# A two-block layer stack on one core: where two weight passes stand between the levels of the recurrent stage's inverse

## The chip, the cores and the metric

The kernel runs on one NeuronCore of one Trainium2 chip. The metric is the device time of one execution in microseconds (us). Of the kernel before, three runs took 3465.11, 3466.57 and 3469.8 us (median 3466.57). One further execution, the profiled one, took 3465.34 us.

## The reference

The program computes one block of a hybrid of dilated attention and an RWKV-7 recurrence with a feed-forward network, and then two layers of another hybrid block; x is 512 tokens by 1024 features in float32. Only the recurrence of the first block matters here. Its inputs are three projections of the same activations, each shifted in time, and its 16 heads run over the 512 tokens:

```python
rwkv_part = token_shift(proj[...], shift_mu[l])      # u + (prev - u) * mu
r_r, r_k_, r_v, dw, da, dg = jnp.split(rwkv_part, cuts, axis=-1)
...
def step(state, inp):
    r_t, w_t, k_t, v_t, a_t, b_t = inp
    sa = jnp.einsum('bhvk,bhk->bhv', state, a_t)
    state = (state * w_t[:, :, None, :] + sa[..., None] * b_t[:, :, None, :]
             + v_t[..., None] * k_t[:, :, None, :])
    return state, jnp.einsum('bhvk,bhk->bhv', state, r_t)
```

r is the receptance, k the keys, v the values. After it each head's output is normalised, gets a bonus term and is multiplied with a gate.

## The kernel before

Features lie on the 128 partitions, the 512 tokens on the free axis. The program is written out by hand for each engine: every engine works through its own list in program order, and semaphores say when an input is there. No scheduler moves anything.

**A weight pass.** `pe_features` (L582) multiplies one tile of 128 output features: 8 products over the 1024 input features, each as three matmuls of 128x512 (L574, L577, L578: weights and activations are each split into a high and a low part), so 24 matmuls. The weights stream in blocks of 8 such tiles. GpSimd (POOL) splits each block (L3293 to L3297) as soon as TensorE (PE) has begun with the block after the one whose buffer it needs, so a split begins some way into a weight pass.

**The recurrent stage.** Two heads make a pair; `pe_rwkv` (L1161), `act_rwkv` (L1710) and `dve_rwkv` (L2513) work on pair j = 0 to 7. Inside a pair the recurrence over 128-token chunks needs the inverse of a triangular matrix, which is built in five levels k = 1 to 5. In each level PE does: products z (L1192, 32 small matmuls), the transposes of the inverse so far (L729), products "normal" (L1192 with `plain`) and then the next level. VectorE (DVE) masks z (L2547) before the second products, and adds the second products to the inverse (L2562) before the next level; ScalarE (ACT) copies the transposes (L1726) before the second products.

**The chain of the pair before.** Into levels 1 to 4 of pair j the four chunk steps of pair j-1 are woven, three parts each: `first` (L1097, L1099), then ACT copies W (L1707), `second` (L1111), ACT copies U (L1707), `third` (L1122 to L1131), ACT copies the output (L1707). Pair 0 has no such chain.

**The inputs of the pair after.** For j = 0 to 6 (`more`) the three weight passes of pair j+1 stand in pair j: keys before level 1, receptance in level 2, value in level 4, the last two between `first` and `second`. ACT copies each result out of PSUM (`act_rwkv_copy`, L1636). Further work of pair j+1 has its place in the lists of the other engines:

- DVE after level 1: the cumulative sums of the decays (step 1, L2420 to L2427). In level 2, between z and the additions: the shift of the keys (step 2, L2754 and L2756), and, from pair 2 on, the mixing of pair j-2 (L2608, L2611). After level 3: step 3 (L2433, L2436). In level 4, between z and the additions: the shift of the receptance (step 4), the reciprocal of the key's length (step 8, L2444 to L2448) and step 9 (L2452). The shift of the values is at the pair's end (step 7).
- ACT in level 2, between W and U: a table load and the exponentials of the decays (`act_rwkv_decays`, L1663 to L1671). After level 3: a table load and the square root of the key's length (L1689).
- PE after level 3: the sum of squares for that length (`pe_rwkv_length`, L637).

Level 5 has the head means and the transposes of three more matrices, and after it the score maps follow (L1154, L1156). In pair 7 gate passes stand in levels 2 and 4; the change does not touch them.

Of the kernel before, what the change touches and what calls it, by code (L numbers as in the profile page):

```python
# [581 lines left out]
def pe_features(pe, ring, tag, act, k=KD, ready=None):  # L582

    tl = pe.tile(ring)
    pe.eng.wait_ge(tl.free, pe.emptied(tl))
    pe_product(pe, tl.ps, tag, *act, k, ready).then_inc(tl.full, pe.up("full_" + ring))
    return tl
# [402 lines left out]
def of(hi, lo, at=0):  # L990

    return (lambda t: hi[:, at + t, :]), (lambda t: lo[:, at + t, :])
# [60 lines left out]
def pe_rwkv_value(pe):  # L1053

    pe_features(pe, "a", "rkv", of(pe.b.h_hi, pe.b.h_lo))
# [105 lines left out]
def pe_rwkv(pe, j, chain):  # L1161

    b = pe.b
    H, AR, TF, LT = of(b.h_hi, b.h_lo), b.R_AR[j % 2], b.R_TF[j % 2], b.R_LM[:, :, 0]
    more = j + 1 < KD
    pe_features(pe, "a", "g2", of(b.s_hi, b.s_lo, 1), 1)
    pe_features(pe, "a", "gate", H)
    pe_features(pe, "d", "branch", of(b.s_hi, b.s_lo, 2), 2)
    pe.eng.wait_ge(pe.sem["rk_ready"], pe.due("rk_ready"))
    pe_plain(pe, "d", b.pair, b.R_T)  # L1170
    pe_rwkv_start(pe, lambda r, c: b.R_BH[r, c * P:(c + 1) * P], lambda r, c: AR[r, c, 0])
    tiles = [pe.tile("d") for _ in range(2)]
    pe.eng.wait_ge(tiles[1].free, pe.emptied(tiles[1]))
    for c in range(NQ):
        for half in ROWS:
            at = slice(c * P + half.start, c * P + half.stop)
            for tl, r in zip(tiles, ROWS):
                m = pe.eng.matmul(tl.ps[half, c * HD:(c + 1) * HD], AR[r, c, 0, half], b.R_BH[r, at],
                                  start=True, stop=True)
                if c == NQ - 1 and half is ROWS[1]:  # L1180
                    m.then_inc(tl.full, pe.up("full_d"))
    if more:
        pe_rwkv_keys(pe, j + 1)
    else:
        pe_features(pe, "a", "gate", H)

    def products(lhsT, rhs):
        tiles = [pe.tile("d") for _ in range(2)]
        pe.eng.wait_ge(tiles[1].free, pe.emptied(tiles[1]))
        for v in range(4):  # L1190
            for n, (row, out) in enumerate(((0, 0), (1, 1), (0, 1), (1, 0))):
                m = pe.eng.matmul(tiles[row].ps[ROWS[out], v * HD:(v + 1) * HD], lhsT(v, row, out), rhs(v, row, out),  # L1192
                                  start=True, stop=True)
                if v == 3 and n >= 2:
                    m.then_inc(tiles[row].full, pe.up("full_d"))
        return tiles[1]

    def block(t, v, row, out):
        return t[ROWS[row], 2 * v + out]

    def diagonal(src):
        tl = pe.tile("d")
        pe.eng.wait_ge(tl.free, pe.emptied(tl))
        for u in range(8):
            for r in ROWS:
                m = pe.eng.matmul(tl.ps[r, u * HD:(u + 1) * HD], src[r, u], b.ident[r, r], start=True, stop=True)
        m.then_inc(tl.full, pe.up("full_d"))
        return tl

    def corner(out, lhsT, rhs):  # L1210
        tl = pe.tile("a")
        pe.eng.wait_ge(tl.free, pe.emptied(tl))
        for u in range(8):
            m = pe.eng.matmul(tl.ps[out, u * HD:(u + 1) * HD], lhsT(u), rhs(u), start=True, stop=True)
        m.then_inc(tl.full, pe.up("full_a"))
        return tl

    for k in range(1, 6):
        c = k - 1 if chain and k <= NQ else None
        if k == 1:  # L1220
            pe.eng.wait_ge(pe.sem["t_ready"], pe.due("t_ready"))
        else:
            pe.eng.wait_ge(normal.free, pe.taken(normal))
        z = products(lambda v, row, out: LT[ROWS[row], 2 * v + out, ROWS[row]], lambda *at: block(b.R_TN, *at))
        inverse = pe_turned(pe, [b.R_TN[:, 2 * v:2 * v + 2].rearrange("p u t -> p (u t)") for v in range(4)])
        if c is not None:
            chain.first(c)
        if k == 2 and more:
            pe_rwkv_receptance(pe)
        if k == 4 and more:  # L1230
            pe_rwkv_value(pe)
        if k in (2, 4) and not more:
            pe_features(pe, "a", "gate", H)
        if k == 5:
            if j:
                pe_rwkv_mean(pe)
        if c is not None:
            chain.second(c)
        pe.eng.wait_ge(inverse.free, pe.taken(inverse))
        pe.eng.wait_ge(z.free, pe.taken(z))  # L1240
        normal = products(lambda *at: block(b.R_TW, *at), lambda *at: block(b.R_Z, *at))
        if k == 5:
            for src in (b.R_V, b.R_BH, b.R_KH):
                turned = pe_turned(pe, [src[:, q * P:(q + 1) * P] for q in range(NQ)])
            pe_rwkv_maps(pe, j, (0, 1))
        if c is not None:
            chain.third(c)
        if k == 3 and more:
            pe_rwkv_length(pe)
    upper, lower = ROWS  # L1250
    pe.eng.wait_ge(normal.free, pe.taken(normal))
    z = corner(lower, lambda u: LT[upper, u, lower], lambda u: b.R_TN[upper, u])
    last = diagonal(b.R_TN)
    maps = pe_rwkv_maps(pe, j, (2, 3))
    pe.eng.wait_ge(last.free, pe.taken(last))
    pe.eng.wait_ge(z.free, pe.taken(z))
    last = corner(upper, lambda u: b.R_Z[lower, u], lambda u: TF[lower, u, HD:])
    if j:
        pe_rwkv_variance(pe)
    return PeChain(pe, j, (turned, maps, last))  # L1260
# [368 lines left out]
def act_rwkv_copy(a, n):  # L1629


    if n - 1 > 0:
        a.eng.wait_ge(a.sem["shifted"], a.value("shifted", n - 1))
    a.eng.wait_ge(a.sem["full_a"], a.due("full_a"))
    a.eng.wait_ge(a.sem[a.last], a.own())
    a.eng.activation(a.b.R_U[:, n % 2, 1:], a.bank(), ACT.Copy).then_inc(a.sem["free_a"], a.up("free_a"))  # L1636
    a.eng.wait_ge(a.sem[a.last], a.own())
    a.eng.sem_inc(a.sem["u_ready"], a.up("u_ready"))
# [71 lines left out]
def act_rwkv(a, j):  # L1710
    b = a.b
    W, U, Y = b.R_WU[:, 0], b.R_WU[:, 1], [b.R_Y[:, c * P:(c + 1) * P] for c in range(NQ)]
    more = j + 1 < KD
    a.eng.wait_ge(a.sem["full_a"], a.due("full_a"))
    a.eng.wait_ge(a.sem[a.last], a.own())
    a.eng.activation(b.R_G[j % 3], a.bank(), ACT.Copy).then_inc(a.sem["free_a"], a.up("free_a"))
    act_first_gate(a, b.x[:, j])
    if more:
        act_rwkv_keys(a, j + 1)
    else:  # L1720
        a.eng.wait_ge(a.sem["rk_ready"], KD)
        act_late_gate(a, 0)
    for k in range(1, NQ + 2):
        a.eng.wait_ge(a.sem["full_a"], a.due("full_a"))
        a.eng.wait_ge(a.sem[a.last], a.own())
        a.eng.activation(b.R_TW, a.bank().rearrange("p (u t) -> p u t", u=8), ACT.Copy).then_inc(a.sem["free_a"], a.up("free_a"))  # L1726
        if k > NQ:
            continue
        if j:
            act_rwkv_chunk(a, W)  # L1730
        if k == 2 and more:
            act_rwkv_decays(a)
            act_rwkv_copy(a, 2 + 3 * (j + 1) + 1)
        if k == 4 and more:
            act_rwkv_copy(a, 2 + 3 * (j + 1) + 2)
        if k in (2, 4) and not more:
            act_late_gate(a, k // 2)
        if j:
            act_rwkv_chunk(a, U)
            act_rwkv_chunk(a, Y[k - 1])  # L1740
        if k == 2 and more:
            act_rwkv_squares(a, j + 1)
        if k == 3 and more:
            act_rwkv_length(a)
    for dst in (b.R_VN, b.R_BN, b.R_KN):
        a.eng.wait_ge(a.sem["full_a"], a.due("full_a"))
        a.eng.wait_ge(a.sem[a.last], a.own())
        a.eng.activation(dst, a.bank().rearrange("p (c n) -> p c n", c=NQ), ACT.Copy)\
            .then_inc(a.sem["free_a"], a.up("free_a"))
    if j:  # L1750
        act_rwkv_centered(a)
    for part, dst in ((slice(HD, P), b.R_Z[HD:P]), (slice(0, HD), b.R_TF[j % 2][0:HD, :, HD:])):
        a.eng.wait_ge(a.sem["full_a"], a.due("full_a"))
        a.eng.wait_ge(a.sem[a.last], a.own())
        a.eng.activation(dst, a.bank()[part].rearrange("p (u t) -> p u t", u=8), ACT.Copy)\
            .then_inc(a.sem["free_a"], a.up("free_a"))
    if j:
        act_rwkv_deviation(a)
# [1627 lines left out]
```

## Time and profile before

| what | value |
|---|---|
| median of 3 runs | 3466.57 us |
| profiled execution | 3465.34 us |
| span of the profile | 3463.4 us |
| mean granted TensorE clock | 0.978 |
| PE busy | 3247.9 us (94%) |
| DVE busy | 2009.3 us (58%) |
| POOL busy | 1674.6 us (48%) |
| ACT busy | 1055.9 us (30%) |
| chain that ended last, by engine | PE 75%, DVE 16%, ACT 5% |
| level 1 of pair 0 to level 1 of pair 7 | 288.94 to 740.81 us |

The span runs from the first to the last instruction; the 1.9 us between it and the execution's own time lie around the program. The recurrent stage is where PE is least the bound: its list, DVE's and ACT's wait for each other level by level.

### The profile page before, as it was taken

What the parts mean: (1) busy time and instruction counts of PE and PEld (TensorE: products, weight loads), DVE (VectorE), ACT (ScalarE), POOL (GpSimd) and SP (SyncE); (2) the same over time, 40 slices, a digit from 0 to 9 for tenths busy, and PEclk for the clock granted to TensorE, in tenths of its full rate; (3) what the DMA queues carried; (4) which work ended last, traced back from release to release, by engine and by line L of the source; (5) the groups of instructions that cost most, each with busy time, mean ns of one, the idle gap of its engine ahead of it and who ended that gap; (6) DMA issues with size and microseconds to landing.
All of it is one profiled execution on the core that took longest, in us unless ns stands there. A gap on an engine that the chain in (4) does not pass through costs nothing.

```text
span 3463.4 us, 52617 instructions
## 1 busy us (share of the span) xinstructions
PE 3247.9 (94%) x19342; PEld 2566.8 (74%) x19342; DVE 2009.3 (58%) x2727; ACT 1055.9 (30%) x1970; POOL 1674.6 (48%) x1323
## 2 busy tenths in 40 slices
PE   7988999899999999899999999999989899999999
PEld 4756777777888887576777788877657677788887
DVE  5647677765566545624645666656552635586556
ACT  2142333322121113543534321112551535231112
POOL 3423322225476664244344666655226263576665
PEclk9998999999999999999999999999999999999999
DMA  5431111112232221012121232222112121222222
GB/s 206 165 121 44 44 38 38 38 38 67 91 100 96 95 95 61 31 55 67 54 69 62 85 98 92 97 86 80 36 37 92 37 86 44 85 90 93 97 96 92
DMA packets 71657, 268.36 MB, mean 77 GB/s; under 512 B 7840, under 2 KB 7968, under 8 KB 68384
## 3 DMA queue, kind: packets, MB, share of 16 engines
q1 hardware_dynamic: 69152, 260.73, 22.6%
q10 hardware_dynamic: 2304, 4.83, 0.4%
q8 instruction: 140, 2.29, 0.3%
q14 instruction: 61, 0.50, 0.0%
HBM read 263.44 MB, written 2.10 MB: 77 GB/s over the span
## 4 chain that ended last, share of the span: by engine, by line
PE 75%; DVE 16%; ACT 5%; issue 2%; DMA 1%; POOL 0%; DVEq 0%; SPq 0%; ACTq 0%; POOLq 0%
PE psum_a L574 10%; PE psum_a L578 10%; PE psum_a L577 10%; PE psum_d L637 5%; PE psum_d L574 5%; PE psum_d L577 5%; PE psum_d L578 5%; PE psum_a L729 3%; PE psum_d L832 2%; PE psum_a L600 2%; PE psum_a L603 2%; PE psum_a L604 2%; PE psum_a L759 1%; PE psum_a L763 1%; PE psum_a L762 1%
## 5 line engine op out<-in xcount | busy, mean ns | idle before, releaser
L3297 POOL TENSOR_TENSOR w_lo<-raw,w_hi 128x1024 fp32r<-128x1024 f32 x440 | 1114.3, 2532 | 36.7
L3293 POOL TENSOR_TENSOR mark<-mark 128x1 f32<-128x1 f32 x438 | 105.5, 241 | 1712.7 <-PE psum_a L574 866.7
L574 PE MATMUL psum_a<-h_hi,w_hi 128*128 128x512 f32 x1712 | 676.7, 395 | 0.0
L578 PE MATMUL psum_a<-h_hi,w_lo 128*128 128x512 f32 x1712 | 669.1, 391 | 0.0
L577 PE MATMUL psum_a<-h_lo,w_hi 128*128 128x512 f32 x1712 | 668.9, 391 | 0.0
L3294 POOL TENSOR_SCALAR w_hi<-raw 128x1024 fp32r<-128x1024 f32 x440 | 471.2, 1071 | 33.8 <-DMA raw<-in_weights 33.8
L574 PEld LDWEIGHTS psum_a<-h_hi,w_hi 128*128 128x128 f32 x1712 | 323.1, 189 | 78.1 <-issue 11.2
L577 PEld LDWEIGHTS psum_a<-h_lo,w_hi 128*128 128x128 f32 x1712 | 323.1, 189 | 68.0 <-issue 1.9
L578 PEld LDWEIGHTS psum_a<-h_hi,w_lo 128*128 128x128 f32 x1712 | 322.7, 189 | 68.0
L574 PE MATMUL psum_d<-split,w_hi 128*128 128x512 f32 x848 | 331.1, 390 | 9.5 <-DVE x L3044 6.7
L577 PE MATMUL psum_d<-split,w_hi 128*128 128x512 f32 x848 | 330.0, 389 | 0.0
L578 PE MATMUL psum_d<-split,w_lo 128*128 128x512 f32 x848 | 330.0, 389 | 0.0
L574 PEld LDWEIGHTS psum_d<-split,w_hi 128*128 128x128 f32 x848 | 159.2, 188 | 47.3 <-issue 13.1
L578 PEld LDWEIGHTS psum_d<-split,w_lo 128*128 128x128 f32 x848 | 159.2, 188 | 33.1
L577 PEld LDWEIGHTS psum_d<-split,w_hi 128*128 128x128 f32 x848 | 159.2, 188 | 32.7
L637 PE MATMUL psum_d<-arena 64*128 64x512 f32 (+4 forms) x480 | 158.7, 579 | 12.2 <-DVEq L2844 6.9
L759 PE MATMUL psum_a<-h_hi,w_hi 128*128 128x256 f32 x416 | 123.8, 297 | 0.0
L729 PE MATMUL psum_a<-const,arena 128*128 128x128 f32 x820 | 117.2, 282 | 2.8 <-DVEq L2973 1.6
L1858 ACT ACTIVATE arena<-arena,col 128x512 f32<-128x512 f32 (+5 forms) x144 | 104.3, 724 | 47.7 <-DVE col L2644 26.4
L763 PE MATMUL psum_a<-h_hi,w_lo 128*128 128x256 f32 x416 | 117.6, 283 | 0.0
L762 PE MATMUL psum_a<-h_lo,w_hi 128*128 128x256 f32 x416 | 117.5, 283 | 0.0
L729 PEld LDWEIGHTS psum_a<-const,arena 128*128 128x128 f32 x820 | 92.7, 143 | 31.1 <-issue 20.0
(394 smaller groups left out, 5713.9 us busy)
## 6 DMA issues: line engine op xcount, KB each, us to landing
raw<-in_weights SPq DMA_DIRECT2D x440, 512.0 KB, 3.4
plain<-in_ada SPq DMA_DIRECT2D x20, 1024.0 KB, 7.2
arena<-in_ada SPq DMA_DIRECT2D x4, 1024.0 KB, 17.5
x<-in_x SPq DMA_DIRECT2D x1, 2048.0 KB, 12.8
x<-in_x ACTq DMA_DIRECT2D x1, 2048.0 KB, 10.7
out<-x SPq DMA_DIRECT2D x8, 256.0 KB, 3.7
arena<-in_pe ACTq DMA_DIRECT2D x2, 512.0 KB, 3.6
const<-in_const ACTq DMA_DIRECT2D x1, 906.0 KB, 9.4
```

The lines of the kernel that those rows point to most:

```text
L574: m = pe.eng.matmul(dst, wh, hi(t), start=t == 0, stop=False)
L577: pe.eng.matmul(dst, wh, lo(t), start=False, stop=False)
L578: m = pe.eng.matmul(dst, wl, hi(t), start=False, stop=t == k - 1)
L637: pe.eng.matmul(tl.ps[0:lhsT.shape[1], 0:rhs.shape[1]], lhsT, rhs, start=True, stop=True)\
L729: m = pe.eng.transpose(tl.ps[:, q * P:(q + 1) * P], s, pe.b.ident)
L759: m = pe.eng.matmul(tl.ps[:, cols], wh, b.h_hi[:, t, cols], start=t == 0, stop=False)
L762: pe.eng.matmul(tl.ps[:, cols], wh, b.h_lo[:, t, cols], start=False, stop=False)
L763: m = pe.eng.matmul(tl.ps[:, cols], wl, b.h_hi[:, t, cols], start=False, stop=t == KD - 1)
L1858: a.eng.activation(u.x, u.x, ACT.Exp, bias=u.neg, scale=1.0 if u.scale is None else u.scale, accum_out=u.sum)\
L3293: eng.tensor_tensor(b.mark[:, 1:2], b.mark[:, 0:1], b.mark[:, 0:1], ALU.add)
L3294: eng.tensor_scalar(hi, b.raw[:, s], 1.0, 0.0, ALU.mult, ALU.add).then_inc(sig["w_high"], 1)
L3297: eng.tensor_tensor(lo, b.raw[:, s], hi.bitcast(F32), ALU.subtract).then_inc(sig["w_ready"], 1)
```

## The change

Receptance's pass goes from level 2 to level 1, value's from level 4 to level 3, in PE's list; the two copies go with them in ACT's list. The decays stay in level 2. DVE's list is not changed, and no instruction is added or removed. The order of the weights in memory is the same, since receptance still comes before value.

```diff
@@ -1225,9 +1225,9 @@
         inverse = pe_turned(pe, [b.R_TN[:, 2 * v:2 * v + 2].rearrange("p u t -> p (u t)") for v in range(4)])
         if c is not None:
             chain.first(c)
-        if k == 2 and more:
+        if k == 1 and more:
             pe_rwkv_receptance(pe)
-        if k == 4 and more:
+        if k == 3 and more:
             pe_rwkv_value(pe)
         if k in (2, 4) and not more:
             pe_features(pe, "a", "gate", H)
@@ -1730,8 +1730,9 @@
             act_rwkv_chunk(a, W)
         if k == 2 and more:
             act_rwkv_decays(a)
+        if k == 1 and more:
             act_rwkv_copy(a, 2 + 3 * (j + 1) + 1)
-        if k == 4 and more:
+        if k == 3 and more:
             act_rwkv_copy(a, 2 + 3 * (j + 1) + 2)
         if k in (2, 4) and not more:
             act_late_gate(a, k // 2)
```

PE's list at level 4 of pair 1 (the level begins with the products z, L1192; L1097 and L1099 are `first`, L1111 is `second`). Before, the value pass follows `first`:

```order
L1192 MATMUL psum_d<-arena 64x64 x16
L729 MATMUL psum_a<-const,arena 128x128 x4
L1097 MATMUL psum_a<-arena 128x128
L1099 MATMUL psum_a<-arena 128x64 x2
L574 MATMUL psum_a<-h_hi,w_hi 128x512
L577 MATMUL psum_a<-h_lo,w_hi 128x512
L578 MATMUL psum_a<-h_hi,w_lo 128x512
```

and of the change, at the same place:

```order
L1192 MATMUL psum_d<-arena 64x64 x16
L729 MATMUL psum_a<-const,arena 128x128 x4
L1097 MATMUL psum_a<-arena 128x128
L1099 MATMUL psum_a<-arena 128x64 x2
L1111 MATMUL psum_a<-arena 128x64 x2
L1192 MATMUL psum_d<-arena,plain 64x64 x16
L1128 MATMUL psum_a<-arena 128x128
```

The pass's 24 matmuls, of which the first three stand in the first piece, are gone from level 4; they now stand between L1099 and L1111 of level 3. The same happens to receptance's pass between levels 2 and 1.

ACT's list at levels 1 and 2 of pair 1 (L1726 copies the transposes, L1707 the chunk results, L1636 a weight pass's result, L1663 to L1671 are the decays). Before:

```order
L1707 ACTIVATE arena<-psum_a 128x128 x3
L1726 ACTIVATE plain<-psum_a 128x512
L1707 ACTIVATE arena<-psum_a 128x128
L1663 ACT_TABLE_LOAD
L1663 ACTIVATE arena<-arena,col 128x128 x4
L1666 ACTIVATE arena<-col 128x4
L1668 ACTIVATE col<-col 128x4
L1671 ACTIVATE arena<-arena,col 128x128 x4
L1636 ACTIVATE arena<-psum_a 128x512
L1707 ACTIVATE arena<-psum_a 128x128 x2
```

and of the change:

```order
L1707 ACTIVATE arena<-psum_a 128x128
L1636 ACTIVATE arena<-psum_a 128x512
L1707 ACTIVATE arena<-psum_a 128x128 x2
L1726 ACTIVATE plain<-psum_a 128x512
L1707 ACTIVATE arena<-psum_a 128x128
L1663 ACT_TABLE_LOAD
L1663 ACTIVATE arena<-arena,col 128x128 x4
L1666 ACTIVATE arena<-col 128x4
L1668 ACTIVATE col<-col 128x4
L1671 ACTIVATE arena<-arena,col 128x128 x4
L1707 ACTIVATE arena<-psum_a 128x128 x2
```

The copy L1636 moved from behind the decays in level 2 to between W and U in level 1; U and the output of level 2 (the last L1707) stand directly behind the decays in both, but for that copy.

## Rows read from the trace of the kernel before

**Rows 1.** Page, part 4: the chain that ended last, by engine.
```profile
PE 75%; DVE 16%; ACT 5%; issue 2%; DMA 1%; POOL 0%; DVEq 0%; SPq 0%; ACTq 0%; POOLq 0%
```

**Rows 2.** Stretches view, level 1 of pair 6, and sum over pairs 1 to 6.
```profile
core 0: us, PE busy (x) PEld busy (x) DVE busy (x) ACT busy (x) POOL busy (x), PEclk, DMA share, GB/s
...
680.16:684.95 4.79, 4.13 (x90) 3.50 (x89) 2.95 (x6) 1.75 (x4) 0.64 (x1) 1.00 0.32 111
sum 28.73, PE 24.76 PEld 20.97 DVE 13.62 ACT 10.50 POOL 8.10; mean PE 4.13 PEld 3.49 DVE 2.27 ACT 1.75 POOL 1.35
```

**Rows 3.** The same, level 3 of pair 6, and sum over pairs 1 to 6.
```profile
695.51:701.60 6.09, 5.72 (x95) 4.27 (x95) 3.85 (x11) 2.83 (x7) 0.00 (x0) 1.00 0.20 75
sum 36.76, PE 34.19 PEld 25.50 DVE 21.98 ACT 17.72 POOL 0.50; mean PE 5.70 PEld 4.25 DVE 3.66 ACT 2.95 POOL 0.08
```

**Rows 4.** The same, level 2: pair 1, and sum over pairs 1 to 6.
```profile
358.23:368.49 10.26, 9.92 (x119) 8.37 (x117) 6.11 (x15) 6.95 (x16) 3.68 (x3) 1.00 0.03 10
...
sum 62.13, PE 59.66 PEld 50.23 DVE 50.69 ACT 42.02 POOL 23.16; mean PE 9.94 PEld 8.37 DVE 8.45 ACT 7.00 POOL 3.86
```

**Rows 5.** The same, level 4: pairs 0 and 3, and sum over pairs 0 to 6.
```profile
304.80:317.85 13.05, 7.38 (x94) 5.94 (x93) 12.19 (x12) 1.79 (x3) 4.38 (x3) 0.90 0.13 41
...
503.66:513.76 10.10, 9.55 (x114) 7.93 (x113) 9.24 (x12) 3.33 (x7) 3.88 (x3) 1.00 0.12 39
...
sum 82.04, PE 64.66 PEld 53.52 DVE 76.03 ACT 21.78 POOL 27.04; mean PE 9.24 PEld 7.65 DVE 10.86 ACT 3.11 POOL 3.86
```

**Rows 6.** Timeline, PE, pair 6, levels 1 and 2.
```profile
start us, us, engine line op out<-in xcount [idle before <-releaser]
...
681.28 0.56 PE L1099 MATMUL psum_a<-arena 128*128 128x64 f32 x4
682.50 0.66 PE L1111 MATMUL psum_a<-arena 128*128 128x64 f32 x4 [0.66 <-ACT arena L1707]
...
686.29 0.56 PE L1099 MATMUL psum_a<-arena 128*128 128x64 f32 x4
686.65 0.48 PE L574 MATMUL psum_a<-h_hi,w_hi 128*128 128x512 f32 x1
...
692.23 0.56 PE L1111 MATMUL psum_a<-arena 128*128 128x64 f32 x4
```

**Rows 7.** Timeline, ACT, pair 6, level 2.
```profile
687.31 1.28 ACT L1663 ACT_TABLE_LOAD   x1
...
690.83 1.71 ACT L1671 ACTIVATE arena<-arena,col 128x128 f32<-128x128 f32 x4
692.65 0.60 ACT L1636 ACTIVATE arena<-psum_a 128x512 f32<-128x512 f32 x1
693.42 0.28 ACT L1707 ACTIVATE arena<-psum_a 128x128 f32<-128x128 f32 x1 [0.17 <-ACTq L1638]
```

**Rows 8.** Timeline, DVE, pair 6, levels 2 and 4.
```profile
691.67 2.74 DVE L2611 TENSOR_TENSOR plain<-arena 128x512 f32<-128x512 f32 x1
...
703.66 0.69 DVE L2754 TENSOR_TENSOR arena<-arena 128x512 f32<-128x512 f32 x1
...
705.71 3.35 DVE L2446 RECIPROCAL arena<-arena 128x512 f32<-128x512 f32 x1
```

**Rows 9.** Timeline, PE, pair 6, level 3 and start of level 5.
```profile
696.95 0.56 PE L1099 MATMUL psum_a<-arena 128*128 128x64 f32 x4
697.87 0.66 PE L1111 MATMUL psum_a<-arena 128*128 128x64 f32 x4 [0.37 <-ACT arena L1707]
...
711.99 0.32 PE L1192 MATMUL psum_d<-arena 64*64 64x64 f32 x5 [0.68 <-DVE arena L2562]
```

**Rows 10.** Waits view, PE, 288 to 735 us: total, times, longest.
```profile
PE psum_d L1192 <- DVE arena L2562: 18.9, 11, 5.7
```

**Rows 11.** Timeline, POOL, pair 6, level 2.
```profile
689.36 0.19 POOL L3293 TENSOR_TENSOR mark<-mark 128x1 f32<-128x1 f32 x1 [8.55 <-PE psum_a L574]
...
691.18 2.69 POOL L3297 TENSOR_TENSOR w_lo<-raw,w_hi 128x1024 fp32r<-128x1024 f32 x1
```

**Rows 12.** Stretches view, pair 0, levels 1 and 2.
```profile
288.94:292.65 3.71, 1.98 (x69) 1.53 (x68) 1.69 (x4) 1.20 (x2) 0.00 (x0) 1.00 0.42 141
292.65:301.09 8.44, 7.38 (x93) 5.94 (x93) 7.20 (x12) 6.45 (x14) 3.93 (x3) 1.00 0.11 31
```

**Rows 13.** The same, first products of level 5, pairs 1, 4 and 5.
```profile
385.68:388.00 2.32, 2.32 (x54) 1.49 (x58) 0.99 (x3) 0.60 (x1) 0.00 (x0) 1.00 0.30 120
...
577.57:581.02 3.45, 3.45 (x39) 1.83 (x39) 0.85 (x2) 0.60 (x1) 0.00 (x0) 0.57 0.19 74
643.33:646.76 3.43, 3.43 (x39) 2.19 (x39) 0.85 (x2) 0.60 (x1) 0.00 (x0) 0.57 0.00 0
```

**Rows 14.** The same, level 5 to the gate pass, pairs 2 and 3.
```profile
451.39:464.67 13.28, 12.48 (x181) 9.13 (x181) 8.12 (x15) 4.07 (x7) 0.00 (x0) 0.87 0.09 35
513.76:525.48 11.72, 10.92 (x181) 8.37 (x181) 8.12 (x15) 4.07 (x7) 0.00 (x0) 1.00 0.04 14
```

## The prediction

> **What bounds the kernel now.** I read the chain of waits by engine first. Over the whole program PE carries 75% of it, but DVE has 16% and ACT 5% [rows 1], and the change touches only the recurrent stage, so the next view is that of stretches, cut at the start of each level's products z. The levels of pairs 1 to 6 are very unlike. A level without a weight pass is short: level 1 has 4.79 us in pair 6 and 28.73 us over six pairs [rows 2], level 3 has 6.09 us [rows 3] (36.76 us over the six; it also holds the length sum). Level 2, with receptance's pass, takes 10.26 us in pair 1 and 62.13 us over six [rows 4]; level 4, with value's, 10.10 to 13.05 us and 82.04 us over pairs 0 to 6 [rows 5]. The pass itself is 5.58 us (686.65 to 692.23 in [rows 6]).
>
> If the pass were all that makes levels 2 and 4 long, moving it would be neutral. So the question is what else is in them, and there the timelines of ACT and DVE decide.
>
> Level 2: ACT does the table load and the decays from 687.31 to 692.54 (690.83 + 1.71), and only then copies receptance's result (692.65) and U (693.42) [rows 7]. PE's pass ends at 692.23 [rows 6]. The two run side by side and end within 0.4 us of each other: either alone would make the level nearly as long.
>
> Level 4: DVE has, between its two visits to PSUM for the inverse, the shift, the reciprocal of 3.35 us and three more operations [rows 8]. Here DVE ends later than PE even with the pass in place: the next level's z waits 0.68 us for DVE's additions in pair 6 [rows 9], and the waits view has 18.9 us of waits on these additions in the stage, the longest 5.7 us [rows 10]. In DVE's busy time the same is seen: 76.03 of 82.04 us [rows 5]. Level 4 is a DVE level; the pass is hidden in it completely.
>
> Levels 1 and 3, where the passes go, have almost nothing to hide them: PE is busy 4.13 of 4.79 us in level 1 [rows 2] and 5.72 of 6.09 in level 3 [rows 3], and the idle time that a pass there could fill is the wait for W before `second`, 0.66 us in level 1 [rows 6] and 0.37 us in level 3 [rows 9].
>
> **The change part by part**, for pairs 1 to 6 at full clock first.
>
> Level 1 gains a pass. Between the starts of `first` and `second` lie 1.22 us now (681.28 to 682.50); with a pass between them it is 5.94 us (686.29 to 692.23) [rows 6], so +4.72 us. The copy of receptance stands before U on ACT, which makes `third` wait about 0.2 us more. +4.9 us each, 29.4 us for six. Behind the wait on ACT is queued only `third` and the next z.
>
> Level 3 gains the other one: 0.92 us (696.95 to 697.87, [rows 9]) becomes 5.94, +5.02, and 0.2 for the copy: +5.2 us each, 31.2 for six. Nothing else of DVE or ACT stands in these levels that the pass could cover; step 1 and step 3 on DVE come after the additions, which wait for PE's second products, so they start late by the same amount.
>
> Level 2 loses its pass, but ACT's decays keep their place between W and U. They depend on the cumulative sums, which start after level 1's additions as before. U now comes directly behind them, at 692.65 in place of 693.42 in pair 6: 0.77 us earlier. So level 2 goes from 10.26 to 9.49 us, and 6 x 9.49 = 56.9 against 62.13: -5.2 us. DVE's path through the level is shorter: masks, shift and mixing without a stall, then the additions, done some 7.7 us after the level's start, so it isn't the one that ends it. As bounds from other rows: no gain at all (10.26), and a bare level 1 (4.79), the latter only if the decays were not in the way, which the order of ACT's list excludes.
>
> Level 4 loses its pass too, and DVE's list is unchanged. The length is that of DVE alone. Pair 3 has it without a stall: 10.10 us [rows 5]. In the other pairs DVE's operations on SBUF sit out POOL's split of a weight block: L2611 takes 2.74 us in [rows 8] where L2754, an operation of the same shape, takes 0.69, and POOL's L3297 ran from 691.18 to 693.87 [rows 11]. The Trainium skill, "SBUF — State Buffer", section "SBUF: two separate sides", calls the port pair that the two engines share an exclusive lock, held for the whole instruction; the trace agrees, since L2611 ends 0.54 us after L3297 and not in proportion to it. A split begins inside a weight pass: here at 689.36, 2.7 us after the pass began, when POOL had waited 8.55 us for PE, and it took 4.5 us to the end of L3297. With the pass in level 3 it falls mostly before level 3's additions, where DVE waits for PE anyway. So I take 10.10 us for all six: 60.6 against 82.04 - 13.05 = 68.99, -8.4 us. Bounds: no return (0) and this.
>
> Pair 0 has no chain, so the pass stands between transposes and second products. Level 1: 3.71 us becomes 8.44, as its level 2 is now [rows 12]: +4.7. Level 2: nothing waits for a U; it is a bare level of 3.71 us, plus about 1.4 by which the cumulative sums hold up DVE's masks, plus about 0.8 by which the key shift (0.69 and 0.75 us) outlasts the second products: 5.9 instead of 8.44, -2.5. Level 3: like level 1, +4.7. Level 4: its 13.05 us are 2.95 above pair 3's [rows 5]; most of that is stalls of DVE, I take -2.7. Together +4.2.
>
> Sum at full clock: 29.4 + 31.2 - 5.2 - 8.4 + 4.2 = +51.2 us.
>
> The clock. PE would now stand idle for about 3.9 us in level 2 (from the end of the second products, some 4.1 us into the level, to `third` at 8.0) and about 5 us in level 4 (from `third`, done after 5.0 us, to 10.1). Before level 5 PE already waits for DVE now. After the shorter waits (pairs 1, 3, 6; 0.68 us in pair 6, [rows 9]) the granted clock stayed at 1.00, that is 2.4 GHz. After the longer ones (pairs 0, 2, 4, 5; up to 5.7 us, [rows 10]) it fell to half, 1.2 GHz: over the first products of level 5 the mean is 1.00 in pair 1 and 0.57 in pairs 4 and 5 [rows 13]. What a fall costs is in [rows 14]: level 5 and what follows takes 13.28 us at a clock of 0.87 (pair 2), 11.72 us at 1.00 (pair 3), so 1.5 us for one fall. New falls: six after the idle time of level 2, which slow the start of level 3, and three in level 5 (pairs 1, 3, 6; the others have paid already). 9 x 1.5 = 13.5 us. Bounds: none, 0; twice as long at half clock each, 27.
>
> The Trainium skill, "TensorE: Matmul & The Clock Gate", section "What's actually happening", says that the throttled state is the default and activity releases it, so a kernel pays for gaps between its matmuls beyond the gaps themselves. A count of PE's work alone, which is the same before and after, would leave the 13.5 us out; the four falls named above agree with the page.
>
> DMA, SP and POOL: the passes keep their order, so the same blocks are loaded and split, only earlier inside a pair; POOL's 8.55 us of waiting before its split [rows 11] are time in hand. Nothing. Pair 7 and all that follows only moves.
>
> Total: 51.2 + 13.5 = 64.7 us. Against the profiled execution's own time, 3465.34 us, that is 3530.0 us. The three timed runs have their median 1.2 us higher, well inside their spread of 4.7, so I leave it at 3530.
>
> **The rivals.**
>
> A. The clock doesn't fall in level 2, or the fall is over before the pass starts, and level 5 pays little more: 51.2 us, 3516. For it: the idle time of level 2 is broken by short products. Against: the waits before level 5 of pairs 4 and 5, shorter than 3.9 us, were enough [rows 13]. 17%.
>
> B. POOL's splits catch DVE again, in step 1 or in the start of level 4, and the clock stays low for longer: the 8.4 us don't come back and the clock costs up to 27: 51.2 + 8.4 + 20 = 80, 3545. For it: the idle time of 5 us in every pair would be as long as pair 0's of 5.7, the longest in the stage now [rows 10]. 15%.
>
> C, the other side. The decays and DVE's operations would end early enough, and the pass was what ended levels 2 and 4. Then each of these levels falls by a full pass, 14 x 5.58 = -78 us in pairs 0 to 6; levels 1 and 3 give 29.4 + 31.2 + 9.4 = +70: 8 us faster, 3457, and below that as far as the 18.9 us of waits for DVE shrink. It decides at one place: whether `third` of level 2 starts within 1 us of the second products' end, or stands behind L1671. For it is only that PE is 75% of the chain; against it are the ACT rows of level 2 and the DVE rows of level 4. 2%.
>
> D. The exchange is nearly neutral, because in levels 1 and 3 the passes fill idle time that the view of stretches doesn't show, PE's busy time being modelled. Then within 7 us of 3466. It would need some 4 us of idle time in each of these levels, where PE's rows leave under 1. 2%.
>
> The forecast, 3530, has the rest, 64%.
>
> **How the numbers follow.** A measurement of this kernel can tell 0.2%, 7 us, from no change. All of the forecast, A and B are far on the slow side: slower 96%; same 2% from D, faster 2% from C. The range leaves out C and D and the far tails: the lower end is A less some 6 us for levels that hide more than I count, 3510; the upper end is B, 3547.
>
> **What would show each step right or wrong.** Level 1 of pairs 1 to 6 at 9.7 us and level 3 at 11.3 us (or more where the clock is half). Level 2 at about 9.5 us, with an idle time before L1122 of more than 3 us released by ACT's L1707, behind L1671. Level 4 at 10.1 us with the wait of L1192 for L2562 at 5 us in each of six pairs, over 30 us in total. DVE operations of 2.7 us gone from level 4. A granted clock of about 0.5 at the start of levels 3 and 5. The forecast is wrong if level 2 falls under 8 us, if level 4 falls under 9, or if the change of the time lies outside pairs 0 to 6.

## The result, and the profile after

The changed kernel takes 3537.35 us (median of 4 runs, 3535.89 to 3540.16); the kernel before, run beside it, 3465.84 us. The ratio is 1.0207, with a 95% interval of 1.0190 to 1.0225: 2% slower. The forecast was 3530 with a range of 3510 to 3547. The profiled span grew from 3463.4 to 3535.5 us, the mean granted clock fell from 0.978 to 0.968, and PE's share of the chain by engine stayed at the 75% of [rows 1]. All of the loss lies in pairs 0 to 6: from level 1 of pair 0 to level 1 of pair 7 it is 523.9 us, against 451.9 before (288.94 to 740.81).

Changed kernel, stretches of one level each. The columns are those of [rows 2]. First level 1 of pair 6, then levels 2 to 5 of pair 3; each sum and mean is over pairs 1 to 6.

```profile
739.95:749.61 9.66, 9.49 (x114) 7.94 (x113) 3.19 (x6) 2.35 (x5) 4.23 (x4) 1.00 0.22 67
sum 57.95, PE 56.94 PEld 47.60 DVE 15.02 ACT 14.10 POOL 28.71; mean PE 9.49 PEld 7.93 DVE 2.50 ACT 2.35 POOL 4.79
...
519.92:530.55 10.63, 5.88 (x94) 4.88 (x92) 7.59 (x18) 6.34 (x15) 0.00 (x0) 0.84 0.05 21
sum 63.81, PE 35.34 PEld 29.32 DVE 44.73 ACT 38.04 POOL 0.91; mean PE 5.89 PEld 4.89 DVE 7.46 ACT 6.34 POOL 0.15
...
530.55:543.22 12.67, 12.50 (x120) 10.14 (x119) 3.13 (x9) 3.60 (x8) 3.59 (x3) 0.87 0.14 43
sum 75.07, PE 73.78 PEld 59.60 DVE 19.20 ACT 21.35 POOL 21.45; mean PE 12.30 PEld 9.93 DVE 3.20 ACT 3.56 POOL 3.58
...
543.22:553.06 9.84, 4.20 (x89) 3.49 (x88) 9.02 (x11) 2.73 (x6) 0.00 (x0) 0.89 0.01 2
sum 60.04, PE 25.16 PEld 20.94 DVE 54.76 ACT 16.66 POOL 0.00; mean PE 4.19 PEld 3.49 DVE 9.13 ACT 2.78 POOL 0.00
...
553.06:566.92 13.86, 13.06 (x180) 9.70 (x181) 8.12 (x15) 4.07 (x7) 0.00 (x0) 0.83 0.01 1
sum 82.60, PE 77.14 PEld 57.27 DVE 48.83 ACT 24.39 POOL 0.00; mean PE 12.86 PEld 9.54 DVE 8.14 ACT 4.07 POOL 0.00
```

Read them against [rows 2] to [rows 5]. Level 1 doubled, from 28.73 to 57.95 us, and is PE from end to end. Level 2 lost 24 us of PE's work (59.66 to 35.34) and got no shorter: 62.13 to 63.81. Level 4 lost 32 us of PE's work (64.66 - 7.38 = 57.28 in pairs 1 to 6 of [rows 5], now 25.16) and gave back 9. Pair 3's granted clock was 1.00 in levels 2 to 5 before; it is now 0.84, 0.87, 0.89 and 0.83.

Changed kernel, waits view of PE, 289 to 807 us (released by; total, times, longest).

```profile
PE psum_d L1192 <- DVE arena L2563: 41.2, 9, 7.3
PE psum_d L1122 <- ACT arena L1707: 24.4, 18, 3.8
```

The first, L2562 before, was 18.9 us in [rows 10]. The second is `third` waiting for ACT's U. Both waits stand in the timeline of PE in pair 3 (columns as in [rows 6]).

```profile
523.44 0.69 PE L1192 MATMUL psum_d<-arena,plain 64*64 64x64 f32 x32 [0.52 <-issue]
527.92 0.79 PE L1122 MATMUL psum_d<-arena 128*128 128x128 f32 x2 [3.79 <-ACT arena L1707]
528.50 0.63 PE L1123 MATMUL psum_d<-arena 128*128 128x128 f32 x2
...
553.06 1.13 PE L1192 MATMUL psum_d<-arena 64*64 64x64 f32 x32 [5.04 <-DVE arena L2563]
```

PE stands idle for 3.79 us in level 2 and for 5.04 us before level 5. What released it is in the other two timelines of the same pair: ACT's decays up to 527.49 and U directly behind them, and DVE's list of level 4.

```profile
525.79 1.70 ACT L1671 ACTIVATE arena<-arena,col 128x128 f32<-128x128 f32 x4
527.59 0.28 ACT L1707 ACTIVATE arena<-psum_a 128x128 f32<-128x128 f32 x1
```

```profile
547.09 3.35 DVE L2447 RECIPROCAL arena<-arena 128x512 f32<-128x512 f32 x1
550.48 0.75 DVE L2449 SCALAR_TENSOR_TENSOR arena<-arena,par 128x512 f32<-128x512 f32 x1
551.27 0.69 DVE L2453 TENSOR_TENSOR arena<-arena 128x512 f32<-128x512 f32 x1
552.06 0.95 DVE L2563 TENSOR_TENSOR arena<-arena,psum_d 128x256 f32<-128x256 f32 x2
```

Changed kernel, stretches of pair 3 that follow the idle time of level 2, and then the start of level 5.

```profile
524.20:527.90 3.70, 0.00 (x0) 0.00 (x0) 3.29 (x6) 3.32 (x10) 0.00 (x0) 0.89 0.00 0
527.90:531.30 3.40, 3.38 (x42) 2.83 (x46) 0.64 (x2) 0.53 (x2) 0.00 (x0) 0.50 0.00 0
531.30:534.70 3.40, 3.40 (x30) 3.14 (x23) 0.85 (x2) 1.35 (x3) 0.00 (x0) 0.62 0.02 5
534.70:543.22 8.52, 8.35 (x74) 6.25 (x73) 2.28 (x7) 1.73 (x4) 3.59 (x3) 1.00 0.20 62
553.06:556.50 3.44, 3.44 (x38) 2.19 (x38) 0.85 (x2) 0.60 (x1) 0.00 (x0) 0.50 0.00 0
556.50:559.90 3.40, 3.40 (x51) 2.76 (x52) 1.53 (x3) 1.20 (x2) 0.00 (x0) 0.81 0.02 5
```

After the idle time the clock is at half, 1.2 GHz, for all of the first 3.4 us and three quarters of the next ((1 - 0.62) x 2). The idle stretch before it, at 0.89, holds another 0.8 us of it ((1 - 0.89) x 2 x 3.70). The half clock covers `third` of level 2 and the beginning of level 3, whose first pass matmul starts at 533.66 (PE's timeline of this pair). A fall in [rows 13] was shorter: 0.57 over 3.45 us is 3.0 us at half, and the next 3.4 us had a mean of 0.94.

### The profile page after: what moved, and what is told of

The parts are those of the page before. It is cut to its first block, busy times and chain, and to the rows that moved or that the text cites. A ratio compares the mean times of both kernels' runs of the same rounds, so it can differ in the third digit from the quotient of the medians.

```text
span 3535.5 us, 52617 instructions
## 1 busy us (share of the span) xinstructions
PE 3268.5 (92%) x19342; PEld 2582.8 (73%) x19342; DVE 1989.1 (56%) x2727; ACT 1055.9 (30%) x1970; POOL 1671.2 (47%) x1323
## 4 chain that ended last, share of the span: by engine, by line
PE 75%; DVE 16%; ACT 5%; issue 2%; DMA 1%; POOL 0%; DVEq 0%; SPq 0%; ACTq 0%; POOLq 0%
PE psum_a L574 10%; PE psum_a L577 10%; PE psum_a L578 10%; PE psum_d L637 5%; PE psum_d L574 5%; PE psum_d L577 4%; PE psum_d L578 4%; PE psum_a L729 3%; PE psum_d L832 2%; PE psum_a L600 2%; PE psum_a L603 2%; PE psum_a L604 2%; PE psum_a L759 1%; PE psum_a L763 1%; PE psum_a L762 1%
## 5 line engine op out<-in xcount | busy, mean ns | idle before, releaser
L3298 POOL TENSOR_TENSOR w_lo<-raw,w_hi 128x1024 fp32r<-128x1024 f32 x440 | 1112.4, 2528 | 36.7
## 6 DMA issues: line engine op xcount, KB each, us to landing
arena<-in_ada SPq DMA_DIRECT2D x4, 1024.0 KB, 17.5
```

What stands on the lines that cost most here:

```text
L3298: eng.tensor_tensor(lo, b.raw[:, s], hi.bitcast(F32), ALU.subtract).then_inc(sig["w_ready"], 1)
```

## The experiments

Ratios are to the kernel before, run on the same chip, with 95% intervals. It had a median of 3467.73 us beside the first four and 3468.51 us beside the last two. Each experiment was one kernel. Where an experiment is said to be some us below the change, that is the difference of the two medians. The kernel before took 1.9 and 2.7 us more beside the experiments than beside the changed kernel; set off against it, the three gains of 18.6, 24.2 and 24 us below are 20.5, 26.1 and 26.8.

**Receptance alone, and value alone.** The first keeps `if k == 4 and more` for value's pass and copy. The second is the kernel before with value's two lines changed:

```diff
-        if k == 4 and more:
+        if k == 3 and more:
             pe_rwkv_value(pe)
```

> Only receptance's pass is moved (level 2 to 1); value's stays in level 4. Theory T (a pass is free only beside a long queue of DVE or ACT, and idle time of PE lowers the clock): level 1 of pairs 1 to 6 at 9.66 us (+29 over six), level 2 at 10.6 (+2), level 3 at 7.5 because it starts at half clock (+9), level 4 unchanged at 11.5 on average, pair 0 +2: about +42 us, 3508. Rival N (the levels trade the pass evenly, level 2 falls by 5.6 us): within 5 us of before, 3466, and the loss of the whole change then lies with value's pass.

> Only value's pass is moved (level 4 to 3); receptance's stays in level 2. Theory T: level 3 of pairs 1 to 6 at 11.3 us at full clock (+31), level 4 at 9.85 (-9), level 5 +6 by the clock, pair 0 +3: about +31 us, 3497, and with the run of receptance alone the two sum to the whole change's 71.5 us within 5. Rival N (level 4 falls by a whole pass): within 5 us of before.

Measured: receptance alone 3509.2 us, ratio 1.0120 (1.0104 to 1.0137), +41.5 us; value alone 3496.0 us, 1.0090 (1.0073 to 1.0107), +28.3 us. Together +69.7 against the whole change's +71.5, well within the intervals: the halves add up, and both came out as expected (3508 and 3497). In receptance alone the half clock at the start of level 3 cost less than the 9 us expected: 42.86 against 36.76 us, +6.1. (The profiled execution of the first was its shortest, 3502.03 us.) Its levels 2 and 4, sums over pairs 1 to 6:

```profile
sum 63.82, PE 35.40 PEld 29.32 DVE 44.76 ACT 38.05 POOL 0.91; mean PE 5.90 PEld 4.89 DVE 7.46 ACT 6.34 POOL 0.15
...
sum 68.96, PE 57.25 PEld 47.58 DVE 63.41 ACT 20.00 POOL 22.66; mean PE 9.54 PEld 7.93 DVE 10.57 ACT 3.33 POOL 3.78
```

Value alone, levels 3 and 4:

```profile
sum 67.77, PE 66.33 PEld 52.10 DVE 23.60 ACT 21.03 POOL 21.99; mean PE 11.05 PEld 8.68 DVE 3.93 ACT 3.50 POOL 3.66
...
sum 60.06, PE 25.16 PEld 20.94 DVE 54.80 ACT 16.69 POOL 0.00; mean PE 4.19 PEld 3.49 DVE 9.13 ACT 2.78 POOL 0.00
```

Level 2 is the changed kernel's to 0.01 us without value's move, and level 4 its to 0.02 us without receptance's. With value's pass still in level 4 DVE is busy 63.41 us there, with it in level 3 54.80: 8.6 us of sitting out POOL's splits, nearly the whole return of level 4 (68.96 - 60.06 = 8.9). And level 3 alone, with no idle time before it in level 2, is 67.77 us where the whole change has 75.07.

**What holds level 2.** ACT's decays move on to level 3, between W and value's copy, so that the pass covers them:

```diff
-        if k == 2 and more:
+        if k == 3 and more:
             act_rwkv_decays(a)
```

> The whole change, and ACT's decays (a table load and ten exponentials, 5.3 us) moved from level 2 to level 3, between W and the copy of the values, beside value's pass. Theory T (the decays between W and U are what holds level 2): U comes 3 us into level 2, DVE's additions at 7.6 us become its end, level 2 at 7.7 in place of 10.6, and level 3 at 11.3 in place of 12.5 if the clock holds: about -25 us against the change, 3512. Rival V (DVE's queue of masks, shift and mixing holds level 2): level 2 stays above 10 us, 3537. Rival P (it is PE's own products at half clock): level 2 stays above 9.

Measured: 3518.74 us, 1.0149 (1.0132 to 1.0166), 18.6 us below the change. Stretch of level 2 in pair 3 and its sum, then two level 3's, of pairs 5 and 6:

```profile
511.15:518.77 7.62, 4.71 (x94) 3.97 (x92) 6.68 (x16) 2.43 (x6) 0.00 (x0) 1.00 0.07 28
sum 44.80, PE 28.27 PEld 23.81 DVE 39.26 ACT 13.85 POOL 0.90; mean PE 4.71 PEld 3.97 DVE 6.54 ACT 2.31 POOL 0.15
...
662.78:677.19 14.41, 13.96 (x118) 11.22 (x118) 4.32 (x12) 7.51 (x17) 3.58 (x3) 0.77 0.11 38
...
741.34:752.67 11.33, 11.05 (x119) 8.71 (x119) 4.16 (x12) 7.52 (x17) 3.58 (x3) 1.00 0.14 48
```

Level 2 fell by 19 us over six pairs: its length was the decays on ACT. The next bound is DVE, seen in PE's timeline of this kernel:

```profile
518.77 0.89 PE L1192 MATMUL psum_d<-arena 64*64 64x64 f32 x32 [1.95 <-DVE arena L2563]
```

The size was missed by some 7 us. Expected was that level 3 would be spared the half clock everywhere (6 x 11.33 = 68.0 us; it took 73.91). It was in pairs 1, 4 and 6 (11.33 us). In pairs 2, 3 and 5 it was not (12.7 to 14.4 us), after a wait of only 1.94 or 1.95 us; pairs 4 and 6 had the same wait and kept their clock.

**What holds level 4.** The reciprocal of the key's length is left out of the computation; a multiplication by a constant stands in its place:

```diff
-        v.eng.reciprocal(b.R_SW, b.R_SW)
+        v.eng.tensor_scalar(b.R_SW, b.R_SW, 1.0 / 256, None, ALU.mult)
```

> The whole change with the reciprocal of the key's length replaced by a multiplication with 1/256 (the reciprocal is left out of the computation): 0.43 us in place of 3.35 on DVE in level 4. Theory T (DVE's queue sets the length of level 4): level 4 at 6.9 in place of 9.85 us in all seven pairs, -20 us, and up to -12 more if the shorter idle time spares level 5 the fall of the clock: 3505 to 3517. Rival C (the chain W, U through ACT, or PE, sets it): level 4 falls by less than 1 us, 3530 or more.

Measured: 3513.17 us, 1.0132 (1.0116 to 1.0149), 24.2 us below the change. Stretches of level 4 and level 5 in pair 3 with their sums:

```profile
530.68:537.60 6.92, 4.19 (x90) 3.49 (x89) 6.10 (x11) 2.73 (x6) 0.00 (x0) 0.99 0.01 2
sum 42.52, PE 25.16 PEld 20.94 DVE 37.24 ACT 16.68 POOL 0.00; mean PE 4.19 PEld 3.49 DVE 6.21 ACT 2.78 POOL 0.00
...
537.60:550.81 13.21, 12.41 (x181) 9.32 (x181) 8.12 (x15) 4.07 (x7) 0.00 (x0) 0.88 0.01 1
sum 82.64, PE 77.17 PEld 57.47 DVE 48.86 ACT 24.40 POOL 0.00; mean PE 12.86 PEld 9.58 DVE 8.14 ACT 4.07 POOL 0.00
```

Each level 4 lost 2.92 us (9.84 to 6.92), as DVE's list did: it is a DVE level. That a shorter wait would spare level 5 the half clock was wrong: 82.64 us, as in the changed kernel (82.60), after this wait in PE's timeline:

```profile
537.60 0.71 PE L1192 MATMUL psum_d<-arena 64*64 64x64 f32 x16 [2.12 <-DVE arena L2563]
```

The seven level 4's gave 20.4 us. Another 4.2 came from the level 3's (81.60 against 85.84 us over pairs 0 to 6), which the edit does not touch: their pass follows the same wait in level 2 (10.64 us again in pairs 1 to 6), but the half clock in them was shorter (granted 0.90 to 0.97 in pairs 1 to 6, 0.86 to 0.90 in the changed kernel). So the price of a fall was not the same in the two executions; why is open.

**What the clock costs.** The changed kernel with matmuls in PE's idle time whose result nobody reads: three of 128x512 before `third` waits for U in level 2 of pairs 1 to 6 (shown here), and, not shown, four before level 5's products wait for DVE in pairs 0 to 6.

```diff
+            for _ in range(3):
+                pe.eng.matmul(new.ps, b.ident, b.const[:, C_MASK4:C_MASK4 + T], start=True, stop=True)
         pe.eng.wait_ge(self.u.free, pe.taken(self.u))
```

> The whole change, and matmuls that nothing reads in PE's idle time of pairs 1 to 6: three of 128x512 before the third part's wait for U in level 2 (some 3 us), and in pairs 0 to 6 four before the wait for DVE's additions at the start of level 5 (some 4 us). Theory T (idle time lowers the clock, and that is worth over 20 us of the 71.5): the granted clock stays at 1.00 in levels 2 to 5, level 2 at 9.5 us (-7 over six), level 3 at 11.2 (-8), level 5 to the gate pass at 11.7 (-12), pair 0 -5: about -32 us against the change, 3505. Rival K (the clock falls in any case or costs nothing, since the others are waited for): no less than 3530. Rival F (the fillers are too long and delay what stands behind them): above 3540.

Measured: 3513.2 us, 1.0127 (1.0111 to 1.0143), 24 us below the change. Stretches of level 2 in pair 2, then of levels 2, 3 and 5 in pair 3:

```profile
440.75:451.24 10.49, 8.91 (x100) 5.68 (x99) 8.21 (x18) 6.34 (x15) 0.91 (x1) 0.84 0.16 52
...
512.25:521.71 9.46, 7.48 (x100) 5.03 (x98) 7.60 (x18) 6.35 (x15) 0.00 (x0) 1.00 0.06 23
521.71:532.86 11.15, 10.98 (x121) 8.67 (x119) 3.13 (x9) 3.61 (x8) 3.59 (x3) 1.00 0.15 48
...
542.71:554.43 11.72, 10.92 (x181) 8.37 (x181) 8.12 (x15) 4.07 (x7) 0.00 (x0) 1.00 0.01 3
```

The wait is still there, and mostly filled: PE is busy 7.48 us instead of 5.88 in level 2 of pair 3, and still idle for 1.01 us before `third`. The six pairs' levels 2, 3 and 5 take 57.79, 67.14 and 71.29 us instead of 63.81, 75.07 and 82.60. That is 25.3 us. The clock stays at 1.00 in all six level 3's, in five of the level 2's (9.46 us each) and in level 5 of pairs 2 to 6; level 5 of pair 1 has 0.97. The exception is level 2 of pair 2. There PE had waited 0.44 us before `second` and 1.14 us before the second products (0.52 us in the other five pairs), and the clock was at half under the fillers themselves:

```profile
445.51 4.54 PE L1122 MATMUL psum_d<-const 128*128 128x512 f32 x6
```

The same row is 2.84 us in pair 3. At half clock the fillers outlasted the wait and made the level 1.03 us longer, which is what rival F had named, in one place of thirteen. The gain is 8 us short of the 32 expected. Half of that is pair 0, expected at -5: its wait in level 2 got no filler, its level 3 still ran at 0.76 (10.83 us), and only 1.1 us came back in its level 5.

**The other way round: the kernel before, with less of DVE in level 4.** If level 4 is DVE's even with the pass in it, work should leave DVE's list there. The last operation of step 8 (0.75 us) and step 9 (0.69 us) move behind level 5's additions:

```diff
-            for step in (4, 8, 9):
+            for step in (4, 8):
...
+        if k == 5 and more:
+            dve_rwkv_input(v, j + 1, 9)
```

> The kernel before, without the change: on DVE the product that ends step 8 and step 9 (0.75 and 0.69 us, both inputs of the pair after) moved from level 4 to behind level 5's additions, where DVE waits about 1.1 us for the first score maps. Theory T (level 4 is as long as DVE's queue in it): the waits before level 5 shorten by up to 1.5 us each, 7 to 8 us over seven pairs, and three falls of the clock may go (4.5 us): 3455 to 3460. Rival M (what leaves level 4 delays the maps by the same amount): 3466, the same. Rival S (the operations meet POOL's splits or hold up the maps and ACT behind them): above 3468.

Measured: 3451.03 us (median of 5), ratio 0.9955 (0.9941 to 0.9969): 17.5 us faster than the kernel before, and the only version that beats both. Stretch of level 4 in pair 1 (five of the six pairs have 9.64 or 9.65, pair 5 has 11.41), and its sum:

```profile
436.36:446.00 9.64, 9.47 (x113) 7.93 (x112) 7.79 (x10) 3.06 (x6) 2.49 (x3) 1.00 0.01 3
sum 59.62, PE 56.92 PEld 47.56 DVE 49.57 ACT 18.62 POOL 21.34; mean PE 9.49 PEld 7.93 DVE 8.26 ACT 3.10 POOL 3.56
```

PE is now busy 9.47 of 9.64 us where before it waited (10.10 without a stall, up to 12.91 with one). Level 4 came down from 68.99 to 59.62 us, as far as the exchange brought it, but with the pass still inside. DVE's busy time in these levels fell by 14.3 us (63.84 to 49.57), of which 8.6 are the two operations' own; the other 5.6 are waits for splits that just these two had sat out (L2448 took up to 2.47 us in place of 0.75, L2452 2.72 in place of 0.69 in pair 2) and that nothing in the level sits out any more. Pair 5's fell on other operations and stayed.

The medians are 17.5 us apart, 4 to 9 us more than was expected; the ratio makes it 15.6. Not all of it is the edit's. In the profiled executions the span shrank by 14.7 us, and 10.7 of that lie in the stage (441.2 us from level 1 of pair 0 to level 1 of pair 7, against 451.9), nearly all in the seven level 4's (82.04 to 71.15). 1.1 us lie before the stage and 2.9 behind it, where the two programs are the same: PE's longest waits there agree within 0.1 us, and some groups of matmuls have a mean 1 or 2% lower (L668 421 ns against 429). That looks like the clock of the execution, which was not tested.

## Why the prediction was right, and which terms were off

From the profiled executions, pairs 1 to 6 unless said otherwise:

| term | predicted | measured |
|---|---|---|
| level 1 | +29.4 | +29.2 |
| level 3, full clock | +31.2 | +30.4 |
| level 2, full clock | -5.2 | -5.4 |
| level 4 | -8.4 | -8.95 |
| pair 0 | +4.2 | +6.7 |
| clock | +13.5 | +21.4 |
| from the gate pass on | 0 | -1.3 |
| sum | +64.7 | +72.0 |

Full clock is read from the kernel with fillers: 67.14 - 36.76 for level 3, and for level 2 six times the 9.46 us of the five pairs that kept 1.00, 56.76 - 62.13. The clock's term is what is above it in levels 2 and 3, 7.05 + 7.9, and 6.4 more in level 5 than before (82.60 - 76.21). Pair 0's extra 2.4 us are clock too: its levels 1, 2 and 4 moved by +4.72, -2.44 and -2.68 (predicted +4.7, -2.5, -2.7), its level 3 by +7.06 instead of +4.7, at a granted clock of 0.76. With value's pass alone moved, the same level 3 took 8.43 us, +4.72.

Right: where the two passes stood, other engines set the length; where they went, nothing did. That `third` of level 2 would stand behind L1671 for over 3 us, that level 4 would be DVE's alone, and that these waits would bring the half clock at the start of levels 3 and 5 came as named. The two halves add up, and of the two experiments that relieve ACT or DVE, each shortens the level where that engine was named and leaves the other's alone (levels 2 and 4 are 44.80 and 60.02 us without the decays in level 2, 63.83 and 42.52 without the reciprocal); rival C, by which the passes ended these levels, is out, and so is D.

Mis-sized: the clock, 13.5 against 21.4, or 23.7 with pair 0. Levels 2 and 3 have 15.0 of it where 9.0 was forecast, level 5 has 6.4 where 4.5 was. Two things were missed. First, [rows 14] gave 1.5 us for one fall, taken from falls that lasted some 3.4 us; after the idle time of level 2 the half clock lasted about twice that (0.8 + 3.4 + 2.6 us in pair 3), and a fall cost (7.05 + 7.9) / 6 = 2.5 us. Rival B had this part right, and the prediction's own bound, 27, held it. Second, the cost was placed behind level 2 only. `third` itself runs at half clock in pair 3: from U to the next z it is 530.55 - 527.92 = 2.63 us, and with it level 2 comes to 10.64 us, longer than the 10.26 before, instead of 9.49. The sign expected for level 2 was therefore not seen in its length, although the kernel with fillers shows it (9.46).

B's other half was wrong but for one place. In level 4 no DVE operation on SBUF but the reciprocal is longer than 1 us any more, and the 8.4 us came back. In pair 2 the split of the value weights reached into the end of level 3. DVE's and POOL's timelines of the changed kernel there:

```profile
466.90 1.29 DVE L2489 TENSOR_SCALAR arena<-arena,col 128x128 f32<-128x128 f32 x1
```

```profile
465.75 2.35 POOL L3298 TENSOR_TENSOR w_lo<-raw,w_hi 128x1024 fp32r<-128x1024 f32 x1
```

L2489 ends 0.09 us after L3298, and this pair's level 4 is 10.85 us instead of 9.84.

The Trainium skill, "TensorE: Matmul & The Clock Gate", section "What's actually happening", has activity as that which releases the throttle. The fillers agree but for one level: the same dependent chain with its waits partly filled by unread work kept 1.00 in 17 of these 18 levels to within 0.03, and was 24 us faster.

## What to carry to other kernels

In this kernel a weight pass in a chain of dependent small products cost its length minus what it covered. Before moving it, ask of each level which engine would set its length without the pass: here ACT's decays and DVE's reciprocal, so the pass was nearly free where it stood and cost nearly its full price one level earlier. When a level is longer than its pass, shorten the other engine's list there, by moving what is not needed until later; that paid 10.7 us in the stage here, and the pass stayed. Idle time of PE cost twice, once by itself and once by the clock behind it, so price a new wait with both, and from the longest fall in the traces rather than from a typical one.

## What the runs showed of the hardware that was not expected

- PE's waits of 1.95 and 2.12 us, in stretches of small matmuls, were followed by the half clock: level 5 took 13.21 us at 0.88 after the one of 2.12 us, 11.72 us at 1.00 without. In the kernel before, one of 2.09 us was (pair 4, 0.57 in [rows 13]) and one of 1.41 us was not (pair 1, 1.00 there); in the kernel with less of DVE in level 4, one of 1.69 us was not. The wait of 1.95 us did so in pairs 3 and 5 and not in pairs 4 and 6 of one kernel; what tells them apart stays open.
- In the kernel with fillers, three unread 128x512 matmuls in a wait of 3.8 us left 1.01 us of it idle and the clock at 1.00 in five pairs of six; four in one of 5.0 us (pairs 1 and 3 to 6) left 1.4 us idle, and level 5 began at full clock. In the sixth pair waits of 0.44 and 1.14 us (0.52 in the others) stood just ahead of the fillers, which then ran at half clock; that the longer wait did it was not tested.
